# A hybrid encoder layer on one core: attention scores as two products over 128 rows instead of three over 64, with the queries' high and low parts stacked on the two halves of the partitions

## What is computed

```python
def gqa_attention(zq, zk, zv, q_norm_g, k_norm_g):     # 8 query heads, 2 key/value heads, width 64
    q = apply_axial_rope(rms_norm(q, q_norm_g), ang_r, ang_c) * ATTN_SCALE
    k = apply_axial_rope(rms_norm(k, k_norm_g), ang_r, ang_c)
    s = jnp.einsum('bqkgd,bskd->bkgqs', qblk, k)
    p = jax.nn.softmax(s, axis=-1)
    return jnp.einsum('bkgqs,bskd->bqkgd', p, v)

def encoder_layer(...):
    z = rms_norm(x, norm1_g) @ w_in                    # pool part | q | k | v
    mix = concatenate([pool_mixer(zp), gqa_attention(zq, zk, zv)])
    x = x + mix @ w_out
    x = x + peer_ffn(rms_norm(x, norm2_g))             # 8 heads, product keys, 16384 experts
```

## Time and profile before

| | us |
|---|---|
| median of 3 runs | 1971.09 |
| lowest and highest run | 1969.82, 1972.81 |
| profiled execution, span from first to last instruction | 1973.0 |
| TensorE busy | 1951.1 (99%) |
| VectorE, ScalarE, GpSimd busy | 1642.5, 977.3, 838.5 |

### The profile page before, as it was taken

The page is one execution under the profiler, slowest core; times in us unless marked ns, Lnnn a source line. Parts: engine busy times, 40 slices in busy tenths (PEclk is TensorE's granted clock), DMA queues, the critical chain, the costliest instruction groups (busy, mean ns, idle before and its releaser), DMA issues.

```text
span 1973.0 us, 28846 instructions
## 1 busy us (share of the span) xinstructions
PE 1951.1 (99%) x10204; PEld 1660.6 (84%) x10204; DVE 1642.5 (83%) x3148; ACT 977.3 (50%) x2043; POOL 838.5 (42%) x588
## 2 busy tenths in 40 slices
PE   8999999999999999999999999999999999999999
PEld 8977998987888888888888888788888888788887
DVE  3866436879999999999977776898988999889898
ACT  4266243324787787787877772332222222223231
POOL 0334102001333333433455655555666566666563
PEclk9999999999999999999999999999999999999999
DMA  6110312225789989989899999999999999999996
GB/s 267 43 36 1 139 54 107 79 88 196 232 301 326 300 311 311 321 296 303 299 378 397 401 411 406 362 343 406 390 405 388 407 401 406 399 407 404 406 399 256
DMA packets 203366, 581.27 MB, mean 295 GB/s; under 512 B 19936, under 2 KB 57184, under 8 KB 201056
## 3 DMA queue, kind: packets, MB, share of 16 engines
q0 software_dynamic: 73728, 268.47, 36.6%
q1 hardware_dynamic: 60192, 180.12, 24.5%
q10 hardware_dynamic: 69312, 130.97, 17.6%
HBM read 505.03 MB, written 74.45 MB: 294 GB/s over the span
## 4 chain that ended last, share of the span: by engine, by line
PE 63%; DMA 17%; DVE 11%; issue 4%; POOL 2%; ACT 2%; SPq 0%; ACTq 0%; DVEq 0%
PE ps L334 19%; PE ps L335 18%; PE ps L336 18%; DMA ring_a<-in_v,expert_ids 7%; PE ps L1516 5%; DMA ring_b<-in_v,expert_ids 5%; DVE sparse L1191 2%; DMA ring_c<-in_v,expert_ids 2%; DMA gel_dram<-arena_b 1%; PE ps L1390 1%; DVE arena_a L1215 1%; DVE v_lo_slots_b L1203 1%; POOL ring_c L833 1%; PE ps L1477 1%; DVE v_lo_slots_a L1203 1%
## 5 line engine op out<-in xcount | busy, mean ns | idle before, releaser
L334 PE MATMUL ps<-v_hi_slots,w_lo 128*128 128x512 f32 x1024 | 399.2, 390 | 2.5 <-DVE w_lo L1221 2.3
L336 PE MATMUL ps<-v_hi_slots,w_lo 128*128 128x512 f32 x1024 | 398.4, 389 | 0.0
L334 PE MATMUL ps<-feat_hi,w_hi 128*128 128x512 f32 (+1 forms) x936 | 360.1, 385 | 1.5 <-DVE w_lo L1093 1.1
L335 PE MATMUL ps<-feat_lo,w_hi 128*128 128x512 f32 (+1 forms) x936 | 351.2, 375 | 0.0
L336 PE MATMUL ps<-feat_hi,w_lo 128*128 128x512 f32 (+1 forms) x936 | 351.0, 375 | 0.0
L722 ACT ACTIVATE w_lo<-arena_a 128x512 fp32r<-128x512 f32 x128 | 81.0, 633 | 493.6 <-DVE arena_a L1215 371.4
L833 POOL DMA_INDIRECT ring_a<-in_u_rows,expert_ids x86 | 123.2, 1432 | 320.4 <-DVE ring_a L1183 186.1
L334 PEld LDWEIGHTS ps<-v_hi_slots,w_lo 128*128 128x128 f32 x1024 | 192.2, 188 | 45.0 <-DVE w_lo L1221 5.3
L336 PEld LDWEIGHTS ps<-v_hi_slots,w_lo 128*128 128x128 f32 x1024 | 192.2, 188 | 40.2
L336 PEld LDWEIGHTS ps<-feat_hi,w_lo 128*128 128x128 f32 x936 | 176.2, 188 | 31.8
L334 PEld LDWEIGHTS ps<-feat_hi,w_hi 128*128 128x128 f32 x936 | 176.6, 189 | 30.9 <-DVE w_lo L1093 1.9
(11 more groups left out here) (223 smaller groups left out, 4469.5 us busy)
## 6 DMA issues: line engine op xcount, KB each, us to landing
arena_a<-in_v ACTq DMA_DIRECT2D x121, 512.0 KB, 7.7
w_raw<-in_uT SPq DMA_DIRECT2D x85, 512.0 KB, 6.5
g_dram<-arena_a ACTq DMA_DIRECT2D x64, 512.0 KB, 8.4
gel_dram<-arena_b ACTq DMA_DIRECT2D x120, 256.0 KB, 5.4
w_raw<-gel_dram SPq DMA_DIRECT2D x120, 256.0 KB, 8.2
arena_a<-in_uT SPq DMA_DIRECT2D x43, 512.0 KB, 6.8
w_raw<-in_w_all SPq DMA_DIRECT2D x16, 1024.0 KB, 5.8
arena_b<-g_dram SPq DMA_DIRECT2D x32, 512.0 KB, 11.8
```

The lines of the kernel that those rows point to most:

```text
L334: nc.tensor.matmul(out, lh, rh, start=first, stop=False)
L335: nc.tensor.matmul(out, lh, rl, start=False, stop=False)
L336: return nc.tensor.matmul(out, ll, rh, start=False, stop=last)
```

## The change

Queries: for head 0 of pair j, `feat_hi[:, j]` now holds the high part on rows 0 to 63 and the low part on rows 64 to 127. For head 1, `feat_lo[:, j]` holds the low part on rows 0 to 63 and the high part on rows 64 to 127. VectorE writes low parts to a staging buffer of two (`q_low`), and a DMA on SyncE's queue moves them to the other half of the partitions. Keys: high and low part of each key head are kept on both halves; a DMA copies them over. A score unit is then two products of 128 rows: the stacked queries times the doubled high keys, and times the doubled low keys (this also adds the low x low term). Copies and subtractions of the flips are issued once for each half of the partitions.

```diff
+        KD_ = at("keys_doubled", 24576 + 2048, 3072, F32R)
-        kTh, kTl = KV_[:, 0:TOK], KV_[:, TOK:2 * TOK]
+        k_doubled = view(KD_, 0, 2, 2, TOK)
+        q_low = view(KV_, 0, 2, TOK)
+        def stack(j, hh):
+            return (FTl if hh else FTh)[:, j, :]
+        def rows_of(hh):
+            return slice(64 * hh, 64 * hh + 64)
 # SyncE, after the loads of w chunks 4 to 6
+            def stack_queries(j):
+                sp.wait_ge(q_lo, 4 * (j + 1))
+                for hh in range(2):
+                    sp.dma_start(stack(j, hh)[rows_of(1 - hh), :].bitcast(F32),
+                                 q_low[rows_of(hh), j % 2, :].bitcast(F32)).then_inc(q_stacked[j], 16)
+            sp.wait_ge(k_lo, 4)
+            for hh in range(2):
+                sp.dma_start(k_doubled[rows_of(1 - hh), :, hh, :].bitcast(F32),
+                             k_doubled[rows_of(hh), :, hh, :].bitcast(F32)).then_inc(k_stacked, 16)
+            stack_queries(0)
             for gi in range(2, 4):
                 sp.wait_ge(pool_mm, 2 * (gi - 1))
                 sp.dma_start(band[:, gi % 2, :, :], io["band"][gi]).then_inc(band_in[gi % 2], 16)
+            for j in range(1, 4):
+                stack_queries(j)
             sp.wait_ge(w_lo, 6)
             load_w(7, 1)
 # ScalarE, flip_out(r)
-                dst, b, ok = (kTh, 6, k_hi) if r == 0 else (FTh[:, r - 1, :], 6 - 2 * (r % 2), q_hi)
-                nc.scalar.activation(dst[:, 0:512], ps[:, b, :], ACT.Copy).then_inc(ok, 1)
-                nc.scalar.activation(dst[:, 512:768], ps[:, b + 1, 0:256], ACT.Copy).then_inc(ok, 1)
+                for b, c in ((0, 512), (1, 256)):
+                    for hh in range(2):
+                        rows, cols = rows_of(hh), slice(b * 512, b * 512 + c)
+                        dst = stack(r - 1, hh)[rows, cols] if r else k_doubled[rows, 0, hh, cols]
+                        nc.scalar.activation(dst, ps[rows, 6 - 2 * (r % 2) + b, 0:c],
+                                             ACT.Copy).then_inc(q_hi if r else k_hi, 1)
 # VectorE, q_rest(r), and the keys' low part in the same manner
-                for i, (b, c) in enumerate(((0, 512), (1, 256))):
-                    dve.wait_ge(q_hi, 2 * (r - 1) + i + 1)
-                    tt(FTl[:, r - 1, b * 512:b * 512 + c], ...)
+                if r >= 3:
+                    dve.wait_ge(q_stacked[r - 3], 32)
+                for b, c in ((0, 512), (1, 256)):
+                    dve.wait_ge(q_hi, 4 * (r - 1) + 2 * b + 2)
+                    for hh in range(2):
+                        rows, cols = rows_of(hh), slice(b * 512, b * 512 + c)
+                        tt(q_low[rows, (r - 1) % 2, cols], ps[rows, 6 - 2 * (r % 2) + b, 0:c],
+                           stack(r - 1, hh)[rows, cols].bitcast(F32), ALU.subtract).then_inc(q_lo, 1)
 # TensorE
-                    pe.wait_ge(q_lo, 8)          # windows(3)
+                    pe.wait_ge(q_lo, 16)
-            pe.wait_ge(k_lo, 2)
-            pe.wait_ge(q_lo, 2)
+            pe.wait_ge(k_stacked, 32)
+                if u == 0:                       # scores(j, u)
+                    pe.wait_ge(q_stacked[j], 32)
-                pe_split_product(ps[:, u % 3, 0:n * P], FTh[rows, j, cols], FTl[rows, j, cols], kTh[rows, keys],
-                                 kTl[rows, keys], True, True).then_inc(qk_mm, 1)
+                mm(ps[:, u % 3, 0:n * P], stack(j, hh)[:, cols], k_doubled[:, 0, hh, keys], start=True, stop=False)
+                mm(ps[:, u % 3, 0:n * P], stack(j, hh)[:, cols], k_doubled[:, 1, hh, keys], start=False, stop=True
+                   ).then_inc(qk_mm, 1)
```

More of the change, by code:

```diff
@@ L282, in build @@
             sem(n) for n in ("a_mul", "a_hi", "a_lo", "v_hi", "v_lo", "a_mm", "acc_done", "acc_ev", "done"))
-        dve_step, zero_v = sem("dve_step"), sem("zero_v")
+        dve_step, zero_v, k_stacked = sem("dve_step"), sem("zero_v"), sem("k_stacked")
+        q_stacked = [sem(f"q_stacked{j}") for j in range(4)]
         y_tiles = (4, 5, 0, 1, 2, 3)
@@ L932, in q_rest @@
             def q_rest(r):
-                for i, (b, c) in enumerate(((0, 512), (1, 256))):
-                    dve.wait_ge(q_hi, 2 * (r - 1) + i + 1)
-                    tt(FTl[:, r - 1, b * 512:b * 512 + c], ps[:, 6 - 2 * (r % 2) + b, 0:c],
-                       FTh[:, r - 1, b * 512:b * 512 + c].bitcast(F32), ALU.subtract).then_inc(q_lo, 1)
+                if r >= 3:
[6 more added lines that the diff above has]
+                           stack(r - 1, hh)[rows, cols].bitcast(F32), ALU.subtract).then_inc(q_lo, 1)
             dve.wait_ge(v_parts, 1)
@@ L941, in _ @@
             for b, c in ((0, 512), (1, 256)):
-                dve.wait_ge(k_hi, b + 1)
-                tt(kTl[:, b * 512:b * 512 + c], ps[:, 6 + b, 0:c], kTh[:, b * 512:b * 512 + c].bitcast(F32),
-                   ALU.subtract).then_inc(k_lo, 1)
+                dve.wait_ge(k_hi, 2 * b + 2)
+                for hh in range(2):
+                    rows, cols = rows_of(hh), slice(b * 512, b * 512 + c)
+                    tt(k_doubled[rows, 1, hh, cols], ps[rows, 6 + b, 0:c], k_doubled[rows, 0, hh, cols].bitcast(F32),
+                       ALU.subtract).then_inc(k_lo, 1)
             q_rest(1)
@@ L1347, in flip_qk @@
                 if r == 2:
-                    pe.wait_ge(k_lo, 2)
+                    pe.wait_ge(k_lo, 4)
                 elif r >= 3:
-                    pe.wait_ge(q_lo, 2 * (r - 2))
+                    pe.wait_ge(q_lo, 4 * (r - 2))
                 col = K_COL if r == 0 else (r - 1) * P
@@ L1378, in scores @@
                 t0, n = SEQ_TILES[q]
-                rows, cols = slice(64 * hh, 64 * hh + 64), slice((t0 + t) * P, (t0 + t + 1) * P)
-                keys = slice(t0 * P, (t0 + n) * P)
+                cols, keys = slice((t0 + t) * P, (t0 + t + 1) * P), slice(t0 * P, (t0 + n) * P)
+                if u == 0:
+                    pe.wait_ge(q_stacked[j], 32)
                 pe.wait_ge(exp_ok, j * NU + (u + 1))
-                pe_split_product(ps[:, u % 3, 0:n * P], FTh[rows, j, cols], FTl[rows, j, cols], kTh[rows, keys],
-                                 kTl[rows, keys], True, True).then_inc(qk_mm, 1)
+                mm(ps[:, u % 3, 0:n * P], stack(j, hh)[:, cols], k_doubled[:, 0, hh, keys], start=True, stop=False)
+                mm(ps[:, u % 3, 0:n * P], stack(j, hh)[:, cols], k_doubled[:, 1, hh, keys], start=False, stop=True
+                   ).then_inc(qk_mm, 1)
             def flip(j, u):
```

## The result

The changed kernel takes 1968.09 us (median of 12 runs, 1966.75 to 1971.45). The kernel before, run beside it, takes 1972.33 (12 runs, 1969.82 to 1974.82). The ratio is 0.998, with a 95% interval of 0.9971 to 0.9988: faster, by 4.2 us, where 8.3 were forecast. The forecast's direction and its whole range held; the time lies above its own range of 1959 to 1967. The profiled execution is the fastest of the 12, 1966.75, with a span of 1964.8.

What follows compares the result with a forecast made beforehand. TensorE, busy 99% of the span, was taken to bound the kernel. Attention's 15.3 us less 3.8 (band load), 1.7 (clock) and 1.5 (fourth flip) gave 8.3 off 1971.1: 1962.8 us, own range 1959 to 1967, whole range 1955 to 1970.

Steps and rivals of the forecast that it cites:

- Part 1, gaps and third product: Attention's score units: two products for three drop the third product and the gaps around 64-row units, saving 21.3 us.
- Part 2, the waits it uncovers: Attention: score products wait for the exponential in three places of a pass, costing some 6.0 us over four passes.
- two engines become the bound: Rival, attention: ScalarE and VectorE set the pace, with exponential waits of 10 us; 1966.8 us, chance 0.10.
- the gaps stay: Rival, attention: gaps belong to starting a group, not to 64 rows, so 8.7 less 7.0; 1969.5 us, chance 0.10.
- Part 3, the band load: Stage before attention: group 2's bands queue behind the copies and land at 114.2, so TensorE stands 3.8 us at windows(2).
- The bound from above: Upper bound on the band load's cost, 8.3 us, if copies between partitions run at half the rate.
- the queue: Rival: group 2's bands crawl behind four copies, TensorE stands at windows(2) and again for k_stacked; slower, 1975, chance 0.08.
- Part 3, the clock: Behind the gap at windows(2) the granted clock falls, costing 1.7 us; bounds 0 and 3.4 (a second fall).
- the fourth flip: Stage before attention: windows(3) waits for all of VectorE's subtractions and starts 1.5 us later; bounds 0 and 3.
- what was costed at nothing: Remaining new work taken as covered: query stacks 1 to 3 land long before their passes; load_w(7) is wanted only later.

Runs made afterwards that it cites:

- e3_three_wide: The changed kernel with a third product of 128 rows in every score unit (low keys added a second time): 1973.53 us.
- e2_band_alone: The changed kernel, but SyncE issues nothing more after the bands of group 2 until they have landed: 1965.78 us.
- e8_after_again: The changed kernel run again with no edit: 1968.31 us.
- e11_keep_warm_twice: The changed kernel with 30 idle products ahead of the wait for group 2's bands and 8 more in the second gap, at windows(3): 1964.62 us.
- e4_halves_only: The kernel before, with only the flips' copies and subtractions issued once for each half of the partitions: 1975.54 us.
- e1_band_first: The changed kernel with group 2's bands issued before the wait for the keys' low parts, group 3's after the first query stack: 1959.63 us.
- e7_keep_warm: The changed kernel with 30 idle products of 128x512 ahead of the wait for the bands of group 2: 1965.39 us.

## Why the prediction came out half

- **Part 1, gaps and third product: right.** 21.3 us were forecast, 12.6 of it the gaps and 8.7 the third product. e3_three_wide gives 12.7 for the 128 rows alone. Where values stand ahead of a score unit all three gaps are gone from the rows. The Trainium skill, TensorEngine Tiling (Array Packing), Key Properties, says that a change of tiling mode drains TensorE. The trace agrees, with 0.09 and 0.10 us at the two changes around a unit of 64 rows; the third gap, 0.11, lay inside the unit.
- **Part 2, the waits it uncovers: right in kind, a little high.** 6.0 us were written, but the prediction's own three waits, 0.6 + 0.5 + 0.1 in each of four passes, add up to 4.8. Measured are 8.7 - 4.5 = 4.2, by difference, with 8.7 the prediction's own price; the rows show eight waits for the exponential at L1415, 2.7 us as idle time, which counts from the modelled ends of the matmuls. Parts 1 and 2 together: 15.3 forecast, 17.2 measured, and 17.9 us for a pass where 18.1 were forecast. With 4.8 the forecast would have been 9.5, farther off: the slip brought it nearer by luck. The rival that the two engines become the bound and the rival that the gaps stay are out.
- **Part 3, the band load: this is the step that failed.** The mechanism was right, the term was sized at half: TensorE was to stand 3.8 us late and is 8.1 late, because the load was to land at 114.2 in the old times and landed at 118.4. The rows split these 4.2 us. SyncE issued the load at 112.8 (111.28 + 1.52), not 110.9: 0.8 of that because the first queries' low parts were ready later (110.8, not 110.0), 1.1 because the two issues ahead took 1.98 (109.30 to 111.28), not 0.86. It then took 5.6 us to land, not 3.3: 1.7 for the DMAs issued behind it (e2_band_alone), and 0.6 for what stood ahead of it. The prediction had priced 1472 KB by two loads of the earlier trace rows, in whose time the DMA engines moved 370 GB/s (110 to 111 us of the kernel before), where they now moved 252, and had counted nothing behind the band's own last byte. The bound from above, 8.3 for copies at half the rate, came near 8.1 by luck: 252 is two thirds of 370, and no term of that bound was the later DMAs or the issues. The mechanism of the rival *the queue* is what happened, at 8.1 instead of the 12.1 that would have turned the sign, and without its second stand, for `k_stacked`. Why the copies run at 252 GB/s stays open.
- As an estimate from the Trainium skill's figure, in DMA: Bandwidth & Descriptors, Anatomy of one DMA, the prediction had 113.6 for that landing, 4.8 us too early: the measurement decides.
- **Part 3, the clock: the first fall right, the second missed.** 1.7 were forecast; `windows(2)` lost 1.6 in this profile and 2.1 in e8_after_again's. The bound from above named a second fall and the sum took it at nothing; it came, at `windows(3)`, and cost 1.4 and 1.6 (e11_keep_warm_twice takes both falls away).
- **Part 3, the fourth flip: 1.5 forecast, 2.5 measured** (e4_halves_only, e1_band_first). The full price of a 128-row instruction was too low for one of 64 rows: four copies take 2.03 us for the 1.56 forecast, and four subtractions 2.34 for 2.02. VectorE also waits 0.54 for the second half copy of flip 3.
- **Sum.** 15.3 - 7.0 was forecast, 17.2 - 13.6 measured: part 3 costs twice its price, and 6.6 us are lost there, of which attention's surplus brings back 1.9.

Of the queues, what was costed at nothing stayed so: neither `load_w(7)` nor the stacks 1 to 3 shows among TensorE's waits.

## What to carry to other kernels

When a change puts DMAs into a queue, look at what stood there on time and now stands behind them, and issue the load with the nearest due time first: here the same change with its band loads first is worth 12.2 us (1959.63 against 1971.88), and 4.2 without. Price a run of queued DMAs by what stands ahead and behind, not by one big load. Don't split a copy by partitions to save work: here it was cheaper to write all rows and let the later DMA overwrite what is wrong.

## What the runs showed of the hardware, unexpected

- A 64-partition copy is dearer in a row than a 128-partition one: 0.60 us from start to start on ScalarE for 512 columns, against 0.50. On VectorE the four subtractions of a flip by halves take 2.34 (128.60 to 130.94), the two over all rows 0.93 (119.14 to 120.07 in the kernel before).
- The clock falls behind short gaps in some executions and not in others. At the same place in stage 1 gaps of 1.91 us (the kernel before) and 1.81 (e8_after_again) were followed by half clock, gaps of 1.73 (the changed kernel) and even 2.05 (e2_band_alone) were not. In front of `windows(3)`, 1.76 us were followed by half clock in e7_keep_warm and by full clock in e1_band_first, where TensorE had run at full clock before in both. No rule is read from this; such a gap costs nothing or 1.4 to 2.8 us, which is part of the spread between runs.
- DMA engines can show a share of 1.00 while moving only 229 to 252 GB/s; the same share went with 355 to 426 in the earlier trace rows.
